# The squares' sum of each RMS norm, moved on TensorE from behind the first weight unit of a phase into the middle of the second

## The reference

```python
def rms_norm(x, gain):
    y = x * lax.rsqrt(jnp.mean(x * x, axis=-1, keepdims=True) + EPS)
    return y * gain

for l in range(2):                                    # first block
    h = rms_norm(x, attn_norm[l])
    x = x + mixer(h @ w_in[l]) @ w_out[l]             # "mix1": attention A, attention B, gated scan C
    hf = rms_norm(x, ffn_norm[l]) @ w_up[l]           # "ffn1"
    x = x + (gelu(conv3(gate(hf))) * val(hf)) @ w_down[l]
for layer in range(2):                                # second block
    x = x + 0.5 * swiglu(rms_norm(x, g[0]))           # "ffn2"
    x = x + mix(rms_norm(x, g[1]))                    # "even" (conv + attention) or "odd" (dilated attention + pooling)
    x = x + 0.5 * swiglu(rms_norm(x, g[2]))           # "ffn2"
```

## Time and profile before

| | |
|---|---|
| median of 3 runs | 1739.1 us (1738.5 to 1739.69) |
| the profiled execution, its own time | 1739.11 us |
| its span, first to last instruction | 1737.3 us |
| TensorE busy | 1663.6 us, 96% of the span |
| VectorE, ScalarE, GpSimd busy | 1212.2, 940.8, 510.7 us |
| mean granted TensorE clock | 0.979 of full |
| transfers | 272.09 MB, 157 GB/s |

### The profile page before, as it was taken

One profiled execution on the slowest core, in us unless ns is written; L12 is line 12 of the kernel. 1 busy time (PEld: TensorE's weight loads), 2 busy tenths in 40 slices (PEclk: granted clock), 3 DMA queues, 4 the chain that ended last, 5 costly groups with the idle time before them and its releaser, 6 DMA issues. The chain is left out here.

```text
span 1737.3 us, 30201 instructions
## 1 busy us (share of the span) xinstructions
PE 1663.6 (96%) x10274; PEld 1452.1 (84%) x10274; DVE 1212.2 (70%) x2026; ACT 940.8 (54%) x1549; POOL 510.7 (29%) x492
## 2 busy tenths in 40 slices
PE   7896999999997999999999998999999999899999
PEld 6785899988876999888889867888888889678888
DVE  5776777756776777667765956777577765867763
ACT  5454566534553666456645655665376644456652
POOL 0040433310222434234421004443144411444430
PEclk9998999999998999999999998999999999999999
DMA  7330465654322566556665303656556655246662
GB/s 255 99 120 25 126 189 181 220 174 146 104 80 62 169 182 206 193 169 186 201 201 156 118 16 110 193 183 218 163 176 190 208 185 166 86 122 188 186 219 96
DMA packets 70494, 272.09 MB, mean 157 GB/s; under 512 B 7824, under 2 KB 8976, under 8 KB 70416
## 3 DMA queue, kind: packets, MB, share of 16 engines
q1 hardware_dynamic: 70416, 271.07, 49.6%
HBM read 269.99 MB, written 1.05 MB: 156 GB/s over the span
## 5 line engine op out<-in xcount | busy, mean ns | idle before, releaser
L828 DVE TENSOR_TENSOR wl<-raw,wh 128x1024 fp32r<-128x1024 f32 (+1 forms) x470 | 619.5, 1318 | 127.4 <-ACT wh L536 121.5
L536 ACT ACTIVATE wh<-raw 128x1024 fp32r<-128x1024 f32 (+1 forms) x470 | 525.9, 1119 | 218.5 <-PE gb L1275 115.9
L1271 PE MATMUL gb<-hx,wh 128*128 128x512 f32 x1512 | 543.9, 399 | 0.0
L1272 PE MATMUL gb<-hx,wl 128*128 128x256 f32 x1512 | 424.9, 281 | 0.0
L1271 PE MATMUL gb<-gux,wh 128*128 128x512 f32 x960 | 341.3, 395 | 0.0
L1271 PEld LDWEIGHTS gb<-hx,wh 128*128 128x128 f32 x1512 | 284.8, 188 | 59.2
L1258 PE MATMUL gb<-hx,wh 128*128 128x256 f32 x1008 | 298.6, 296 | 18.3 <-DVE hx L845 10.1
L1272 PEld LDWEIGHTS gb<-hx,wl 128*128 128x128 f32 x1512 | 286.4, 189 | 7.6
L1259 PE MATMUL gb<-hx,wh 128*128 128x256 f32 x1008 | 287.9, 286 | 0.0
L1260 PE MATMUL gb<-hx,wl 128*128 128x256 f32 x1008 | 287.4, 285 | 0.0
L1272 PE MATMUL gb<-gux,wl 128*128 128x256 f32 x960 | 268.5, 280 | 0.0
(11 more groups left out here) (213 smaller groups left out, 2051.7 us busy)
## 6 DMA issues: line engine op xcount, KB each, us to landing
raw<-in_wa SPq DMA_DIRECT2D x374, 512.0 KB, 3.6
raw<-in_wb SPq DMA_DIRECT2D x96, 704.0 KB, 4.2
x<-in_x SPq DMA_DIRECT2D x2, 512.0 KB, 6.1
out_x<-x SPq DMA_DIRECT2D x8, 128.0 KB, 3.1
row<-in_row SPq DMA_DIRECT2D x1, 836.0 KB, 11.4
tab<-in_bias SPq DMA_DIRECT2D x3, 256.0 KB, 4.4
con<-in_const SPq DMA_DIRECT2D x1, 544.0 KB, 8.5
tab<-in_bias SPq DMA_DIRECT2D x1, 512.0 KB, 5.4
```

The source lines that it names most:

```text
L536: nc.scalar.activation(wh[:, slot, 0:nt * P], raw[:, slot, 0:nt * P], ACT.Copy).then_inc(s_hi, 1)
L828: nc.vector.tensor_tensor(wl[:, slot, 0:nt * P], raw[:, slot, 0:nt * P], wh[:, slot, 0:nt * P].bitcast(f32), ALU.subtract).then_inc(s_lo, 1)
L1271: nc.tensor.matmul(bank[:, :], a, both(k), start=start and k == 0, stop=False)
L1272: nc.tensor.matmul(bank[:, 0:SEQ], b, high(k), start=False, stop=False)
```

## The change

On TensorE, `norm(n)` of the phases 1 to 9 no longer stands behind the first unit. It is called inside the phase's second unit, ahead of that unit's block 4 of 0 to 7, in all three kinds of place: the mixers' second unit (`tiles`) and the second unit of ffn1 and ffn2 (`joined`). Phase 0 stays as it is. On ScalarE, the request for the Ln and Exp table set is left out in the phases behind mix1 and odd (n = 1, 3, 9); there are three such requests fewer. Nothing of the computation changes.

```diff
+        SUM_AT = 4
+
...
             def norm(n):
-                roots()
+                if n == 0 or PHASES[n - 1][0] not in ("mix1", "odd"):
+                    roots()
                 act.wait_ge(s_ss, n + 1)
...
-                norm(n)
+                if n == 0:
+                    norm(n)
+
+            def sum_within(n):
+
+                return lambda k: norm(n) if k == SUM_AT else None
...
-                        tiles(i, i % RING, gb[bank_of(kind, u)][:, 0:SEQ], DC, lambda k: mc(hh, k), lambda k: mc(hl, k), True, True)
+                        tiles(i, i % RING, gb[bank_of(kind, u)][:, 0:SEQ], DC, lambda k: mc(hh, k), lambda k: mc(hl, k), True, True,
+                              sum_within(n) if n and u == 1 else None)
...
-                            joined(i, slot, bank, DC, both_h, lambda c: mc(hh, c), True, True)
+                            joined(i, slot, bank, DC, both_h, lambda c: mc(hh, c), True, True,
+                                   sum_within(n) if first and j == 0 else None)
```

## The result

The changed kernel took 1741.66 us in the median of 19 executions, the kernel before 1738.5 us in 19 on the same chip: a ratio of 1.0024, 95% interval [1.0016, 1.0032], so slower, by a quarter of a percent. A second comparison gave 1.0028 [1.0018, 1.0037]. As lengths, ratio times 1738.5, that is +4.2 us [2.8, 5.6] and +4.9 us [3.1, 6.4], where +1.1 us was forecast. The predicted time of 1740.3 us is 1.4 us under the median and the median lies in the stated range, but that is partly luck: the kernel before had a median of 1738.5 us here, not 1739.1. The two kernels differ by some four times the forecast difference, and the sign is certain.

A forecast was written before the change was run, and what follows sets the result against it. TensorE, busy 96% of the span, was taken to bound the kernel. The terms -0.6 + 1.44 + 0.3 = +1.1 us on 1739.1 us gave 1740.3 us, range 1738.1 to 1742.3 us.

The forecast's parts named there:

- the one on the FFNs: Phases 1, 3, 4, 6, 7, 9: rstd 1.3 us later, 2.3 us to spare at unit 4 in phase 1; cost nothing.
- Rival 3: FFNs: pair 0 comes too late for unit 4, at worst 1.3 us in six phases, 1748 us; chance 0.05.
- The wait for acc: Phases 1, 3, 6, 9: TensorE's wait for GpSimd's last add into acc goes, 4 x 0.15 = 0.6 us gained.
- the product's own move: Phases 1 to 9: the ones-product costs TensorE the same inside a unit as at the boundary; nothing, nine times.
- Phase 2: mix1: VectorE's split goes ahead of GpSimd's squares, which take 1.95 us, so the sum is late; 1.44 us lost.
- Rival 1: Phase 2's squares aren't blocked, or even hides its delay; about 0, 1739.2 us; chance 0.22 together with rival 5, no effect.
- Even: Phase 5, where VectorE sets the pace: ScalarE's split of unit 6 comes later; 0.3 us lost.
- odd: Phase 8: y chunk 1 has 1.72 us to spare against 1.09 us of delay; cost nothing.
- the swiglu phases: Swiglu FFNs: more to spare than phase 1's 2.3 us before unit 4; cost nothing.
- the table loads: ScalarE, phases 1, 3, 9: three loads left out, covered by 1.56 us of idle behind them in phase 1; worth nothing.
- rival 2: The clock: delay shifts stalls, one slow stretch fewer gives 1738.6 us, one more 1742.0; chance 0.26, half to each side.

The follow-up runs named there:

- The delay kernels: Kernel before with one or two more ones-products ahead of the real one in phases 1 and 3; 1.0006 and 1.0012.
- the run with the squares first: Changed kernel, VectorE's split in phase 2 waiting until GpSimd's first squares are done; 1739.6 us in one execution.
- the phases from 4 on: Kernel before with the ones-product moved to block 4 in phases 4 to 9 only, table loads kept; 0.9991.
- ffn1 alone: Kernel before with the ones-product moved to block 4 in phases 1 and 3 only, table loads kept; 1.0019, then 1.0023.
- the loads alone: Kernel before with only the three table loads left out, nothing moved; 1.0011.
- phase 2 alone: Kernel before with the ones-product moved to block 4 in phase 2 only, table loads kept; 1.0013.
- one delay: Kernel before with one more ones-product ahead of the real one in phases 1 and 3; 1.0006, +1.0 us.
- two delays: Kernel before with two more ones-products ahead of the real one in phases 1 and 3; 1.0012, +2.1 us.
- the block 1 kernel: Ones-product ahead of block 1 in phases 1, 3, 6 and 9, elsewhere as in the kernel before, three loads left out; 0.9999.
- the one with all that gains: Ones-product at block 1 in phases 1, 3, block 4 in 4, 6, 7, 9, elsewhere as in the kernel before, loads left out; 0.9998.

## Why the prediction was wrong

**The step that failed** is the one on the FFNs, "Cost nothing, with 0.9 us left." (2.3 less 1.3 is 1.0, a slip without weight.) It took unit 4 as the next thing that TensorE needs from the late side, and that reading was right: no profile of the changed kernel has a gap there. But the cost isn't settled at the first reader. In ffn1's loop the side engines wait for each other and never for TensorE, so they can't catch up: the lateness is carried through all 22 pairs whole and meets TensorE again where the second matrix multiplies by the last hidden value, in the last block of its second unit. There 0.66 us were to spare, not the 2.3 us of unit 4, and the lateness against TensorE was 1.39 us. The predicted 1.3 us was near that: rstd itself came 1.16 us later in its phase (1.46 less the 0.30 of start) and TensorE, with its wait and part of the product's price saved, 0.23 us earlier. Cost +1.77 us in two phases. The experiments show it from three sides: only ffn1 moved, the wait is there; at block 2 or 1 it is gone, with 0.32 us to spare at block 1, which is 0.66 less one block's 0.35; at block 6 it is 1.05 us. The row that would have told it, GpSimd's L525 at 332.23 against its reader at 334.36, was in the trace before. Rival 3 had the sign and the kind of mechanism, too late in the FFNs, but the wrong reader, and it expected all six FFNs: the four swiglu ones lose nothing, since their side engines wait for TensorE in each pair.

**The wait for acc** (-0.6) went, and **the product's own move** was costed at nothing. Together they measured -1.3 us. The five phases that had no such wait gained 0.03 to 0.1 us by the move alone, so as an estimate some 0.2 us of the 0.27 in each of the other four is the wait, for 0.15 forecast, and the rest the move. From L1275 to L1275 around it, it is 0.78 us where two blocks without it are 0.35 apart, so the product costs 0.43 us inside the unit, against the 0.51 us worked out for a boundary. The delay kernels' 0.43 us for each repeated product agree.

**Phase 2** (+1.44) was right in place and order, and near in size: L565 was 1.07 us idle, the squares took 1.95 us, the sum's loss was 1.55 us. That the order makes 0.9 us of it is shown by the run with the squares first. The squares took 1.04 us alone in that run and 1.95 us behind a split at block 2, which agrees with what the Trainium skill, "SBUF — State Buffer", section "Who interferes with whom", states: issue order decides which of the two is blocked. Rival 1 is out.

**Even** (+0.3) measured +0.26. **odd**, the swiglu phases and **the table loads** (nothing) were right, as far as the traces show.

**The clock** (rival 2) isn't ruled out as a part of the difference. Its stretches moved TensorE's starts by 1 to 3 us between profiles, and rival 2 put one more slow stretch at 1742.0 us, near the measured 1741.66.

**What stays open.** The terms make +2.3 us and the timings say +4.2 and +4.9. By parts: phase 2 measures +2.3 [0.5, 3.8] for 1.55 seen, the phases from 4 on -1.6 [-3.1, 0.0] for -0.5 seen, the loads +1.9 [-0.5, 4.2] for none, and these agree. The ffn1 part measures +3.3 [1.2, 5.2] and +4.0 [2.1, 5.9] for 1.2 seen, and there some 2 us aren't accounted for. Four traces, two of the changed kernel and two of ffn1 alone, show waits for L527 within 0.2 us of each other; whether they are longer in the executions whose traces weren't kept isn't known.

The largest difference outside the terms lies in the tail of phase 2's mixer. Against the first profile of the kernel before, TensorE loses 3.2 and 2.3 us there in the two profiles of the changed kernel and 2.1 and 1.9 in those of ffn1 alone, and the clock is at half for 20.5 to 23.9 us between 500 and 566 us, where both profiles of the kernel before have 17.1. But the kernel with the loads alone (2.3 us), phase 2 alone (1.9) and one delay (2.3) lose it too, and two delays and the phases from 4 on don't. So it isn't tied to the moved product, and that it makes the missing 2 us isn't shown.

A line fitted to time against mean granted clock, with a level for each kernel, over all 257 executions, doesn't settle it either. At equal clock it puts ffn1 alone at +3.1 us, but two delays at +3.6 for 1.7 seen. It puts the block 1 kernel at -1.1 [-1.6, -0.6] for -1.0 seen and the one with all that gains at -0.7 [-1.2, -0.2], which hints at a gain that the plain timings can't show.

## What to carry to other kernels

When a scalar or a factor becomes late at the head of a loop, don't stop at its first reader. Ask whether the side engines wait for the bound engine inside the loop. Where they do (about 1 us, twice a pair, in the swiglu FFNs) the lateness was gone by the third pair. Where they wait only for each other, at a step as long as the bound engine's (ffn1), it arrived whole at the end, so look there for the reader with the least to spare behind the last iteration. Before moving a small product to save its wait, compare what the wait costs (0.15 us by the rows here) with what becomes late by the move (1.4 us here). A place one block in, instead of four, kept the saving and lost nothing, though its gain is too small to be measured here.

## What the runs showed of the hardware

- The same fp32 ones-product costs TensorE 0.43 us of its starts' spacing in the middle of a unit and 0.51 us by the rows at a boundary between two units; repeated back to back, 0.41 to 0.43 us each.
- ScalarE's table load took 1.28 us, and the activation behind it began 0.01 us after its end.
- GpSimd's 128x512 squares took 1.04 us alone and 1.95 us when VectorE's 128x1024 subtraction had started 0.15 us before them; the subtraction then kept its 1.22 us. In every case here one of the two paid: with the squares first, the subtraction stretched to 1.99 us, or was made to wait.
- Over the 257 executions of all these kernels, the time fell by 1.0 us for each 0.001 of mean granted clock, with 0.8 us left unexplained; the kernel before alone ran from 1733.5 to 1741.8 us. At equal mean clock the changed kernel is 3.1 us slower than before, [2.8, 3.5], so a quarter to a third of the timed difference goes with a slightly lower clock.
